# One step of a two-layer decoder: the third chunk of the attention's input product in three groups, two attention items among them, and two steps of the item loop moved

## The reference

```python
proj = h @ w_qkv                       # (tokens, 1024) @ (1024, 1536): 16 query, 4 key, 4 value heads of 64
q = rope_partial(rmsnorm(q, q_norm), pos)
k = rope_partial(rmsnorm(k, k_norm), pos)
s = einsum(q, k) * 64 ** -0.5          # each block of 128 queries against its own and the block before
m = maximum(s.max(-1), sink)
p = exp(s - m)
denom = p.sum(-1) + exp(sink - m)
o = einsum(p / denom, v)
y = o @ w_out
```

## Time and profile before

| | |
|---|---|
| three runs | 1193.08 us median, 1192.41 to 1193.56 |
| profiled execution | 1195.07 us, its span 1193.2 us |
| TensorE busy | 1176.5 us of the span, 99% |
| VectorE, ScalarE, GpSimd busy | 887.4, 631.7 and 172.7 us |
| granted TensorE clock | 0.998 of full speed |
| chain that ended last | 83% TensorE, 7% VectorE, 3% ScalarE, 3% DMA, 2% issue |

### The profile page before, as it was taken

One profiled execution on the slowest core, in us unless ns is written; L12 is line 12 of the kernel. 1 busy time (PEld: TensorE's weight loads), 2 busy tenths in 40 slices (PEclk: granted clock), 3 DMA queues, 4 the chain that ended last, 5 costly groups with the idle time before them and its releaser, 6 DMA issues.

```text
span 1193.2 us, 24075 instructions
## 1 busy us (share of the span) xinstructions
PE 1176.5 (99%) x9572; PEld 892.4 (75%) x9572; DVE 887.4 (74%) x1327; ACT 631.7 (53%) x1051; POOL 172.7 (14%) x289
## 2 busy tenths in 40 slices
PE   8999999999999999999999999999999999999998
PEld 6865777877777777777774456777777777787886
DVE  5887677586888878777774479757788878787655
ACT  6446455366555555454445469846555555544432
POOL 2000010002223222000003300000222222210001
PEclk9999999999999999999999999999999999999999
DMA  9605453235555455445646310023656456345663
GB/s 283 181 2 159 119 154 95 76 104 153 151 132 144 113 131 149 122 122 146 155 111 228 102 53 2 3 71 108 167 126 162 110 126 155 88 127 140 158 174 78
DMA packets 197626, 148.60 MB, mean 125 GB/s; under 512 B 5905, under 2 KB 178763, under 8 KB 197474
## 3 DMA queue, kind: packets, MB, share of 16 engines
q1 hardware_dynamic: 181392, 101.72, 29.5%
q0 software_dynamic: 16064, 45.68, 16.6%
q10 hardware_dynamic: 90, 0.09, 0.0%
HBM read 109.15 MB, written 9.86 MB: 100 GB/s over the span
## 4 chain that ended last, share of the span: by engine, by line
PE 83%; DVE 7%; DMA 3%; ACT 3%; issue 2%; SPq 1%; DVEq 0%; ACTq 0%; POOLq 0%
PE PS L653 33%; PE PS L875 17%; PE PS L809 15%; PE PS L669 6%; PE PS L1603 3%; DMA stage<-in_w_ffn_up 1%; DMA stage<-stage 1%; DVE wL L363 1%; DVE P L2904 1%; SPq L2954 1%; DVE xT L701 1%; DVE st L2885 1%; DMA rowsF<-in_ffn_conv_b 1%; PE PS L1775 1%; ACT ntmp L709 1%
## 5 line engine op out<-in xcount | busy, mean ns | idle before, releaser
L875 PE MATMUL PS<-hidH,blk 128*128 128x288 f16 x1232 | 227.9, 286 | 0.4 <-ACT val L598 0.4
L363 DVE SCALAR_TENSOR_TENSOR wL<-stage,wH 128x1024 f16<-128x1024 f32 x136 | 165.1, 1219 | 51.6 <-ACT wH L357 51.1
L357 ACT ACTIVATE wH<-stage 128x1024 f16<-128x1024 f32 x136 | 142.0, 1048 | 91.1 <-PE PS L653 50.4
L875 PE MATMUL PS<-hidL,blk 128*128 128x288 f16 x616 | 176.2, 286 | 0.0
L653 PE MATMUL PS<-zH,wH 128*128 128x288 f16 x832 | 169.9, 286 | 0.7 <-DVE zL L714 0.7
L653 PE MATMUL PS<-zL,wH 128*128 128x288 f16 x832 | 169.8, 286 | 0.0
L653 PE MATMUL PS<-zH,wL 128*128 128x288 f16 x832 | 169.8, 286 | 0.0
L875 PEld LDWEIGHTS PS<-hidH,blk 128*128 128x128 f16 x1232 | 120.5, 98 | 30.9 <-ACT val L598 0.7
L653 PEld LDWEIGHTS PS<-zH,wH 128*128 128x128 f16 x832 | 81.2, 98 | 22.0 <-DVE zL L714 1.3
L653 PEld LDWEIGHTS PS<-zH,wL 128*128 128x128 f16 x832 | 81.4, 98 | 20.5
L653 PEld LDWEIGHTS PS<-zL,wH 128*128 128x128 f16 x832 | 81.4, 98 | 20.5
(11 more groups left out here) (487 smaller groups left out, 2550.1 us busy)
## 6 DMA issues: line engine op xcount, KB each, us to landing
stage<-in_w_ffn_up SPq DMA_DIRECT2D x88, 512.0 KB, 4.3
quart<-in_w_ffn_down SPq DMA_DIRECT2D x32, 704.0 KB, 5.4
stage<-stage POOLq DMA_DIRECT2D x54, 256.0 KB, 4.9
stage<-in_w_mlstm_in SPq DMA_DIRECT2D x20, 512.0 KB, 6.4
stage<-in_w_swa_qkv SPq DMA_DIRECT2D x12, 512.0 KB, 4.7
quart<-quart POOLq DMA_DIRECT2D x8, 704.0 KB, 5.3
quart<-mixed POOLq DMA_DIRECT2D x8, 704.0 KB, 5.6
C<-in_state_mlstm_C POOLq DMA_DIRECT2D x4, 1024.0 KB, 6.7
```

Of the source, the lines that this page charges most:

```text
L357: nc.scalar.activation(wH[:, slot, :], stage[:, slot, :], ACT.Copy, scale=WSCALE).then_inc(hi_ready, inc)
L363: nc.vector.scalar_tensor_tensor(out=wL[:, slot, :], in0=stage[:, slot, :], scalar=WSCALE, in1=wH[:, slot, :], op0=ALU.mult, op1=ALU.subtr ...
L875: m = nc.tensor.matmul(down_bank(g), blk[:, g % RING, a, 128 * k:128 * (k + 1)], (hidH, hidL)[b][:, k, HIDDEN[j], :], start=(k == 0 and (a ...
```

## The change

Work is neither added nor left out, but moved, on three engines.

1. The third chunk no longer runs unit by unit over all five tiles. TensorE does all units for tiles 0, 1 and 2, with groups 2 to 6 between them, then groups 7 to 9, then all units for tile 3 with item 0's scores after unit 0, then all units for tile 4 with item 1's scores after unit 1.
2. ScalarE and VectorE follow: maxima, exponentials and division of items 0 and 1 stand around the work on tiles 3 and 4. The weight splits for the output product's units 0 and 1, which stood inside the third chunk, now come after tile 3; the split for unit 2 goes from the chunk's end to item 16.
3. ScalarE copies groups 0 and 1 ahead of the last split of chunk 1, groups 2 and 3 come directly behind `rms(1)`. `rms(2)` moves from behind the exponentials of item 1 to behind those of item 2, and group 13 is turned after item 0's turn.
4. The copy of the samples' queries (group 16) goes ahead of the exponentials of item 10 on ScalarE.
5. VectorE divides item 16 ahead of the maxima of item 17, the last ones.

```diff
-        BEFORE_UNIT = ((0, 1), (2, 3), (4, 5, 6), (7, 8, 9), (10, 11, 12, 13))
+        BEFORE_UNIT = ((0, 1), (2, 3), (4, 5, 6), (7, 8, 9), (10, 11, 12))
+        EARLY_TILES = (0, 1, 2)
+        SAMPLES_TURNED = 9
-        LATE_SPLIT = NI - 1
+        LATE_SPLITS = {NI - 2: 2, NI - 1: 3}
@@ TensorE: the product of one unit is now a function over a list of tiles, qkv_unit(c, u, tiles)
+            for c in range(2):
+                for u in range(4):
+                    qkv_unit(c, u, range(TT))
+            for u in range(4):
+                for g in BEFORE_UNIT[u] if u < 3 else ():
+                    group(g)
+                qkv_unit(2, u, EARLY_TILES)
+            for g in BEFORE_UNIT[3]:
+                group(g)
+            pe.wait_ge(masks_in, 1)
+            for u in range(4):
+                qkv_unit(2, u, (3,))
+                if u == 0:
+                    scores(0)
+            for u in range(4):
+                qkv_unit(2, u, (4,))
+                if u == 1:
+                    scores(1)
-            scores(0)
-            scores(1)
...
                 turn(x)
+                if x == 0:
+                    group(13)
@@ ScalarE
+                for tt in range(TT):
+                    qkv_tile(c, tt)
+                for g in BEFORE_UNIT[0] if c else ():
+                    group_evac(act, g)
+                split_act(act, ahead(unit("qkv", c, 3)))
+            rms(1)
+            for u in range(1, 3):
+                for g in BEFORE_UNIT[u]:
+                    group_evac(act, g)
+            act.wait_ge(asem["rope"], 2)
+            for tt in EARLY_TILES:
+                qkv_tile(2, tt)
+            for g in BEFORE_UNIT[3]:
+                group_evac(act, g)
+            exps(0)
+            qkv_tile(2, 3)
+            split_act(act, ahead(unit("qkv", 2, 0)))
+            split_act(act, ahead(unit("qkv", 2, 1)))
+            exps(1)
+            qkv_tile(2, 4)
...
-            rms(2)
             group_evac(act, 12)
             for x in range(NI):
                 if x == 1:
                     group_evac(act, 13)
+                    rms(2)
...
+                if x + 1 == SAMPLES_TURNED:
+                    group_evac(act, BESIDE_ITEM[SAMPLES_TURNED])
                 if x + 2 < NI:
                     exps(x + 2)
@@ VectorE
+            for tt in EARLY_TILES:
+                qkv_tile(tt)
+                squares_summed(tt)
+            maxima(0)
+            normalise(0)
+            qkv_tile(3)
+            squares_summed(3)
+            split_dve(dve, ahead(unit("qkv", 2, 0)))
+            maxima(1)
+            split_dve(dve, ahead(unit("qkv", 2, 1)))
+            normalise(1)
+            qkv_tile(4)
...
-            maxima(0)
-            maxima(1)
-            squares_summed(3)
             squares_summed(4).then_inc(asem["rss"], 1)
-            normalise(0)
             for x in range(NI):
-                if x == LATE_SPLIT:
-                    split_dve(dve, ahead(unit("qkv", 2, 3)))
+                if x in LATE_SPLITS:
+                    split_dve(dve, ahead(unit("qkv", 2, LATE_SPLITS[x])))
+                if x == NI - 3:
+                    normalise(x + 1)
                     maxima(x + 2)
```

More of the change, by code:

```diff
@@ L2297, in rms @@
                 m.then_inc(asem["rs"], 1)
[L2299 to L2329, removed]
             def exps(x):
@@ L2348, in exps, with qkv_tile @@
                 nc.scalar.activation(s[:, 5, :], s[:, 3, :], ACT.Exp).then_inc(asem["e"], 1)
+            def qkv_tile(c, tt):
+                normed_cols = 256 if c == 0 else 512
+                tm_done(act, "qkv", c, tt)
+                r = ROWS[tt]
+                for part in range(len(tm_parts(tt))):
+                    src, dst, cols = qkv_part(c, tt, part)
+                    wide = min(normed_cols, cols.stop) - cols.start
+                    if wide > 0:
+                        m = nc.scalar.activation(sqx(tt)[0:r, cols.start:cols.start + wide], tm_parts(tt)[part][0][:, 0:wide],
+                                                 ACT.Square, scale=rcol[0:r, tt:tt + 1])
+                    if c < 2:
+                        m = nc.scalar.activation(dst, src, ACT.Copy, scale=rcol[0:r, tt:tt + 1])
+                m.then_inc(asem["sq"] if c == 2 else free["qkv"], 1)
+            act.wait_ge(asem["cz"], 2)
+            for c in range(2):
+                for u in range(3):
+                    if c and u == 0:
+                        rms(c - 1)
+                    split_act(act, ahead(unit("qkv", c, u)))
+                    if c == 0 and u == 0:
+                        column_rstd()
+                if c:
+                    act.wait_ge(asem["rope"], c)
+                for tt in range(TT):
[18 more added lines that the diff above has]
+            qkv_tile(2, 4)
             def out_high(x):
@@ L2905, in normalise, with qkv_tile @@
                                             ALU.mult).then_inc(asem["p"], 1)
+            def qkv_tile(tt):
+                dve.wait_ge(asem["sq"], tt + 1)
+                for part in range(len(tm_parts(tt))):
+                    src, dst, _ = qkv_part(2, tt, part)
+                    m = nc.vector.tensor_scalar(dst, src, rcol[0:ROWS[tt], tt:tt + 1], None, ALU.mult)
+                m.then_inc(free["qkv"], 1)
+            steps = iter(())
+            for c in range(2):
+                next(steps, None)
+                for u in range(4):
+                    split_dve(dve, ahead(unit("qkv", c, u)))
+                    next(steps, None)
+                steps = norm_rope(c)
+                if c == 0:
+                    dve.wait_ge(dMask, 16)
+                    nc.vector.tensor_copy(mask16[:, :], masks).then_inc(masks_in, 1)
+            for _ in steps:
+                pass
+            for tt in EARLY_TILES:
[10 more added lines that the diff above has]
+            qkv_tile(4)
             def scaled(x):
```

90 lines of the change are left out of this document (31 added, 59 removed).

## The result

The changed kernel takes 1194.86 us (median of 20 runs, 1192.6 to 1198.56), the kernel before beside it 1193.0 us (median of 20, 1190.81 to 1194.3). The ratio is 1.0017, 95% interval 1.0011 to 1.0024: slower by 1.3 to 2.9 us. The forecast was 1193.7 us with 1191.2 to 1195.3 around it: within 0.2%, and slower rather than faster. The measured time lies in that range, and just outside the walk's own, 1192.8 to 1194.8. The profiled execution took 1193.2 us, its span 1191.4 us.

The account below looks back on a forecast made before the run. TensorE's work (1176.5 us busy) and its waits were taken to bound the kernel; 1.4 - 0.2 - 0.8 + 0.2 = +0.6 us on the median gave 1193.7 us, with 8 in 10 within 1191.2 to 1195.3.

Parts of the forecast that it names:

- the walk: Main case, 61%: the changed order followed link by link through chunk, items and end; 1193.7 us, own range 1192.8 to 1194.8.
- The wait at group 5: Third chunk: TensorE waits a new 1.75 us for ScalarE's copy of group 2, which stands behind `rms(1)`.
- the rival that it costs nothing (20%): Group 5: the keys' copies come in time, TensorE is 1.75 us sooner; 1191.9, down to 1190.5 us; chance 20%.
- Items 2 and 3: First items: item 2's division 0.8 us late at 715.5, item 3's at 719.5 against 718.10; cost 1.4 us.
- The shift stays: Behind item 3's division: VectorE goes on at 3.4 us an item in both kernels, so the 1.4 us delay lasts.
- The samples' queries: Ahead of item 12's scores: the 0.62 us wait goes, item 10's multiplication is the next limit; gain 0.2 us.
- The last division: Item 16's turn: its division ends at 769.2, before TensorE comes, so the 0.80 us wait goes; gain 0.8 us.
- the cost of 0.2 at item 17: Item 17's division has new splits ahead of it and ends at 777.1, TensorE is there at 776.9.
- The sum: Whole kernel: 1.4 - 0.2 - 0.8 + 0.2 = +0.6 us, added to the median: 1193.7 us.
- the clock: Behind the 1.75 us wait TensorE falls to 1.2 GHz, up to 7.8 us more, 1198 or above; chance 2%.
- a split in the way: Slower rival, 11%: second split or tile 4's squares delay item 1's exponentials, 1.2 us each; 1194.9 to 1196.1 us.

Follow-up runs that it names:

- the upper heap: The changed kernel run again unchanged, 1195.23 us, ratio 1.0017: of its 11 runs' spans, 3 at 1196.1 to 1196.7 us, the other 8 at 1192.2 to 1194.3.
- the second profile of the changed kernel: Profile of the changed kernel run again byte for byte: stretch 108.00 us against 106.39 in its first profile; that set of runs took 1195.23 us, ratio 1.0017.
- two such moves on ScalarE: Against the changed kernel, groups 2 and 3 copied ahead of `rms(1)`, and `rms(2)` ahead of item 2's exponentials; both together 1192.01 us, ratio 0.998.
- the wait of 3.57 us: The changed kernel with three more unused 512-column copies on ScalarE between `rms(1)` and group 2's copy: 1198.66 us (six runs), ratio 1.0032.
- the three in which turns filled it: The changed kernel with 14 turns in TensorE's wait, 1194.94 us; with 17, 1193.43 us; with three more ScalarE copies and 32 turns, 1196.5 us.

## Why the prediction was nearly right, and where it fell short

**The wait at group 5** was forecast at 1.75 us and is 2.01. `rms(1)` came where the walk had it (686.5); TensorE came to the group some 0.3 us sooner than the walk, at 682.22 + 2.84 = 685.06 for group 4's turns where 685.35 stood, and began unit 2 0.14 later (685.25 + 2.84 = 688.1 in place of 687.95). The copies ahead of `rms(1)` took away this wait and 2.21 us: the rival that it costs nothing (20%) is excluded for this order of ScalarE.

The Trainium skill (TensorE: Matmul & The Clock Gate, section "Architectural detail: the array is 16× 32×32, not 1× 128×128") has ScalarE as a strict first-in-first-out queue. The trace agrees: ScalarE idles 4.25 us until 683.69, though TensorE had turned group 2 from 677.87 on, and the copy of it stood behind `rms(1)`.

**Items 2 and 3**: item 2's division forecast at 715.5, measured 715.7; item 3's 719.5 and 719.6. The cost up to there is 1.5 us, forecast 1.4. That both `rms(2)` and VectorE would be limits at item 3 was in the walk ("VectorE is ready at 719.5 as well"), and taking `rms(2)` away gave only 0.4 to 0.5 of its 0.74. "The shift stays" holds as well: VectorE's division of item 11 is 1.56 late (747.08 + 2.84 against 748.36).

**The samples' queries**: forecast a gain of 0.2 with the next limit at item 10's multiplication. The waits did that: 0.62 became 0.17 with a new 0.23 at just that place. But almost nothing of these 0.22 lasts. TensorE turns item 9 1.56 late, item 10 1.43 and item 11 again 1.52 (748.76 + 2.84 against 750.08), since VectorE, which the edit doesn't touch, divides item 11 as late as ever. The kernel with the two late edits alone keeps 0.03.

**The last division**: forecast a gain of 0.8. TensorE's turn of item 16 is 0.90 late where item 15's was 1.52: a gain of 0.62, as the wait fell from 0.80 to 0.18. ScalarE's copy of item 15's turned P ends later than the division; the walk looked at one releaser of this turn and not at the second. Of the cost of 0.2 at item 17, 0.14 came: from item 16's turn to the end of the stretch it is 10.17 us (769.28 to 779.45), before 10.03 (771.22 to 781.25), and TensorE's load of weights for item 17's turn waits 0.2 us for its division.

**The sum** was +0.6 and is +1.04 in the trace at full clock. The terms measured are 1.52 for the first items, nothing for the samples' queries, -0.62 and +0.14 for the end: 1.04. Against the forecast's 1.4 - 0.2 - 0.8 + 0.2 the two gains were each taken 0.2 too large, both for the same reason: the walk stopped one limit too early, before item 11's division in the one case and ScalarE's copy in the other.

**The failed step is the clock.** The text gave it 2% and argued from 3.5 us of waits "in pieces" at full clock. But the longest of those pieces is 0.88 us, and the change makes one of 2 us: no row spoke for full clock behind such a wait. It also priced the fall as if it lasted through units 2 and 3 (7.8 us); it lasts 3.4 us and costs 1.6. How much of the loss is its, the runs don't say. The medians differ by 1.9, with 1.3 to 2.9 possible. If it came in 3 of 11 executions, as the upper heap would have it, it adds some 0.4 to the trace's 1.04, about 1.5 together; if in 4 of 5, as in the profiles, 1.3, and 2.3 together. Both fit. That the range held the time was luck in part: its upper end was drawn for a split in the way, which did not happen, while the walk, with the clock at nothing, ended 1.2 us below the measured 1194.86.

The Trainium skill (same page, section "HAM oscillation — how this bites in real kernels") warns of idle gaps of TensorE, in a kernel whose waits for transfers were some 3 to 5 us each. The wait here is 2.01 us; behind it the clock fell in the second profile of the changed kernel and not in the first.

**Never tested**: what decides whether the clock falls behind a wait of 2.0 us, and in what share of the runs it does.

## What to carry to other kernels

Where an engine waits for a late result, look whether work that others wait for stands behind that wait and could stand ahead of it: two such moves on ScalarE were worth 2.2 and 0.5 us here and turned a slower kernel into a faster one. Walk each wait to all of its releasers, not to the one that comes last today: both late edits left 0.2 to 0.4 us of the wait to the next one, and of the first edit's gain nothing reached the end. And price a new idle time of TensorE as its length plus, with a chance of its own, a fall of the clock; look for evidence in traces with an idle time of about that length, not in a sum of short ones.

## What the runs showed of the hardware

A single wait of 2.0 us, in a stretch where TensorE was otherwise at full clock, was followed in some executions by 3.4 us at half clock (0.50), and in others of the same program not at all. Read in steps of 0.1 us, the half clock lasts 3.4 us in each of the four profiles that have it, but its beginning has no fixed place: 1.5 us after TensorE had work again in the changed kernel's second profile (689.8, the wait ended at 688.27), 1.6 after in the kernel with `rms(2)` early (688.5 and 686.83), 0.5 after in the one without edits 4 and 5 (687.8 and 687.29), and 0.2 before the end of the wait of 3.57 us (689.0 and 689.20). The fall was there in four of the five profiles with an empty wait of 2.0 us or more, and in none of the three in which turns filled it; eight executions are few. It cost 1.61 us behind the 2.0 us wait, and 1.41 behind the one of 3.57.
